# First chunk of the input projection: modulation accumulated as columns, weight splits between the norm pairs, products by pair of row tiles

## What is computed

```python
mod = jax.nn.silu(c) @ w_ada + b_ada                 # (1, 1024) @ (1024, 3072)
shift, scale, gate = jnp.split(mod, 3, axis=-1)
h = _rmsnorm(x, g_pre) * (1.0 + scale[:, None, :]) + shift[:, None, :]
proj = h @ w_in
...
h_sb = ... * jax.nn.silu(sb_z)
y = jnp.concatenate([h_ml, h_sb], axis=-1) @ w_out
x = x + gate[:, None, :] * _rmsnorm(y, g_post)
```

## Time and profile before

| | |
|---|---|
| device time, median of 3 runs | 3646.36 us (3642.9 to 3648.1) |
| the profiled execution: its own time | 3643.63 us |
| the profiled execution: span | 3641.8 us |
| PE busy | 3490.5 us, 96% |
| PEld / DVE / ACT / POOL busy | 77% / 69% / 53% / 18% |
| mean granted TensorE clock | 0.982 |

### The profile page before, as it was taken

How to read it: one execution, slowest core, us unless ns; L and a number is a source line. 1 busy time by engine, 2 the same in 40 slices (tenths; PEclk the granted TensorE clock), 3 DMA queues, 4 the chain that set the end, 5 groups by cost and what they waited for, 6 DMA issues and landing times. The chain is left out here.

```text
span 3641.8 us, 66405 instructions
## 1 busy us (share of the span) xinstructions
PE 3490.5 (96%) x24179; PEld 2821.4 (77%) x24179; DVE 2497.0 (69%) x3508; ACT 1945.8 (53%) x4047; POOL 639.7 (18%) x676
## 2 busy tenths in 40 slices
PE   6998999999999989989999999899999999799998
PEld 4776888999999968867776777677777777688887
DVE  4664445434588862339897999799889888466665
ACT  4453213222344442227776777677777777355554
POOL 1332333000000014401113111210010001223332
PEclk9998999999999999989999999999999999899999
DMA  8888779767856689960011110210011000666664
GB/s 275 313 300 314 261 246 315 262 226 232 295 179 186 193 271 317 307 208 21 25 47 51 47 33 26 70 42 29 26 59 42 12 17 28 182 201 198 206 201 133
DMA packets 415584, 582.24 MB, mean 160 GB/s; under 512 B 35568, under 2 KB 298096, under 8 KB 414288
## 3 DMA queue, kind: packets, MB, share of 16 engines
q1 hardware_dynamic: 398352, 519.86, 43.7%
q0 software_dynamic: 16960, 58.73, 4.7%
HBM read 393.74 MB, written 184.75 MB: 159 GB/s over the span
## 5 line engine op out<-in xcount | busy, mean ns | idle before, releaser
L1399 DVE TENSOR_TENSOR_SCAN a_prod<-a_keep,a_prod,a_zeros 128x512 f32<-128x512 f32 x896 | 1076.8, 1268 | 87.9 <-ACT a_keep L1315 86.8
L1324 ACT COPY a_turned<-a_rt 128x512 f32<-128x512 f32 x1088 | 547.1, 588 | 257.5 <-PE a_rt L1269 257.2
L1315 ACT ACTIVATE a_keep<-a_z 128x512 f32<-128x512 f32 (+3 forms) x1152 | 555.5, 573 | 43.1 <-PE a_z L1258 42.9
L1269 PEld LDWEIGHTS a_rt<-a_ident,a_prod 128*128 128x128 f32 x4224 | 453.8, 141 | 133.7 <-issue 61.2
L1269 PE MATMUL a_rt<-a_ident,a_prod 128*128 128x128 f32 x4224 | 533.5, 279 | 24.3 <-DVE a_prod L1399 23.4
L1280 PE MATMUL a_acc<-a_turned,a_dw 128*64 128x256 f32 x4352 | 520.0, 380 | 0.7 <-ACT a_osum L1334 0.7
L1280 PEld LDWEIGHTS a_acc<-a_turned,a_dw 128*64 128x64 f32 x4352 | 286.7, 136 | 213.7 <-issue 92.6
L1258 PE MATMUL a_z<-a_khi,a_q 64*128 64x512 f32 (+3 forms) x2304 | 374.0, 403 | 1.3 <-DVE a_xe L1385 0.9
L883 DVE TENSOR_TENSOR p_hlo<-p_wraw,p_hlo 128x1024 fp32r<-128x1024 f32 x85 | 104.5, 1230 | 323.7 <-ACT p_hlo L654 323.7
L654 ACT CAST p_hlo<-p_wraw 128x1024 fp32r<-128x1024 f32 x85 | 89.1, 1048 | 393.2 <-PE p_bank L524 209.6
L1399 DVE TENSOR_TENSOR_SCAN a_prod<-a_keep,a_zeros 128x384 f32<-128x384 f32 (+3 forms) x256 | 227.3, 946 | 77.9 <-POOL a_keep L1216 77.9
(11 more groups left out here) (286 smaller groups left out, 6323.3 us busy)
## 6 DMA issues: line engine op xcount, KB each, us to landing
p_hlo<-scratch_parts SPq DMA_DIRECT2D x130, 512.0 KB, 5.0
p_wraw<-scratch_sums SPq DMA_DIRECT2D x128, 512.0 KB, 6.4
p_aslot<-scratch_parts SPq DMA_DIRECT2D x62, 512.0 KB, 5.0
p_wraw<-in_x SPq DMA_DIRECT2D x8, 2048.0 KB, 12.7
p_u<-in_w_in POOLq DMA_DIRECT2D x64, 256.0 KB, 6.1
scratch_wsums<-p_u POOLq DMA_DIRECT2D x32, 512.0 KB, 6.4
p_hraw<-scratch_sbv POOLq DMA_DIRECT2D x32, 512.0 KB, 7.3
m_xt<-in_x SPq DMA_DIRECT2D x32, 512.0 KB, 4.9
```

The lines of the kernel that those rows point to most:

```text
L1269: last = pe.transpose(rt[k % RB][:, h * QW + i * P:h * QW + (i + 1) * P], prod[:, u % PB, 2 * i + h, kb * P:(kb + 1) * P], ident[:])
L1315: act.activation(keep[:, at % KB, 0:w], z[at % ZB][:, 0:w], ACT.Sigmoid, scale=-Z_SCALE).then_inc(keep_done, 1)
L1324: act.copy(by_head(turned[:, k % TB]), by_head(rt[k % RB][:])).then_inc(turned_done, 1)
L1399: dve.tensor_tensor_scan(prod[:, u % PB, s, 0:w][:, ::-1], keep[:, at % KB, 0:w][:, ::-1], zeros[:, 0:w], first, ALU.mult, ALU.add).then_i ...
```

## The change

- **Modulation as columns.** The matmuls swap their operands: the stationary operand is a 128x128 block of `w_ada`, the moving one a single column of silu(c), and the 16 columns of shift and scale are accumulated over k in bank 7 itself. Four matmuls per row tile become sixteen. The rows, their four copies on ACT (L674), the sixteen column matmuls (L449) and POOL's `one` go away. PE makes row tiles 0 to 5 of the modulation, turns x tiles 0 to 3, makes 6 and 7, and turns 4 to 6, then 7.
- **Weight splits between the pairs.** ACT casts two tiles of `wg` behind each `high_norm`, DVE makes two of `gl` behind each `low_norm`, and DVE's `spread` of a pair is moved ahead of the `low_norm` of the pair before it.
- **Products by pair.** Chunk 0's products run pair by pair over banks 0 to 3 at once. Blocks 0 to 3 are all finished in the last pair; chunk 1 is turned two tiles behind blocks 1 and 3 and two at a time around the gate products, which are split into their high and their low half.
- **Order of loads and waits.** SP loads chunk 1 of x ahead of the small tables, and DVE waits for those tables only at chunk 0's gates.

```diff
@@ -292,6 +291,8 @@
             sp.dma_start(wgraw[:, :, 0:8], w_in[:, C_G:C_G + 8].rearrange("(k p) n -> p k n", p=P), allow_slow_non_contiguous=True).then_inc(wgt_in, 16)
+            sp.wait_ge(xn_done, TPC)
+            sp.dma_start(xt, chunks_of_x(x)[1]).then_inc(x_in, 16)
             sp.dma_start(cw[:], conv_w.rearrange("j (m p) -> p j m", p=P), allow_slow_non_contiguous=True).then_inc(small_in, 16)
@@ -347,8 +348,6 @@
 
-            sp.wait_ge(xn_done, TPC)
-            sp.dma_start(xt, chunks_of_x(x)[1]).then_inc(x_in, 16)
             store_parts(0)
@@ -422,14 +421,14 @@
         def _(pe):
-            pe.wait_ge(csil_ready, 2)
-            rows = lambda b: slice(32 * b, 32 * b + 1)
-            for k in range(KT):
+            pe.wait_ge(csil_ready, 1)
+
+            def modulation(k):
                 pe.wait_ge(wada_in[k], 32)
-                for b in range(4):
-                    last = pe.matmul(bank[6][rows(b), :], csil[:, k:k + 1], wada[:, b // 2, k, b % 2 * CH:(b % 2 + 1) * CH],
-                                     start=k == 0, stop=k == KT - 1, skip_group_check=True)
-                last.then_inc(mod_done, 1)
+                for col in range(2 * KT):
+                    last = pe.matmul(bank[7][:, col:col + 1], wada[:, col // KT, k, col % KT * P:(col % KT + 1) * P], csil[:, k:k + 1],
+                                     start=k == 0 and col == 0, stop=k == KT - 1, skip_group_check=True)
+                return last
 
@@ -442,35 +441,65 @@
 
-            for k in range(RING):
+            for k in range(6):
+                modulation(k)
+            for k in range(4):
                 turn(0, k)
-            pe.wait_ge(row_ready, 5)
-            for k in range(2 * KT):
-                last = pe.matmul(bank[7][:, k:k + 1], mrow[0:1, k * P:(k + 1) * P], one[:], start=True, stop=True)
-            last.then_inc(col_done, 1)
-            turn(0, 6)
+            modulation(6)
+            modulation(7).then_inc(col_done, 1)
+            for k in range(4, 7):
+                turn(0, k)
             pe.wait_ge(col_ready, 3)
             turn(0, 7)
-            for n in range(NCH):
+
+            def gate_products(n, k, low):
+                dst = bank[(BLOCKS * n + 4) % RING]
+                if low:
+                    return pe.matmul(dst[0:8, :], wgt[:, k, 0:8], hlo[:, n % 2, k], start=False, stop=k == KT - 1, skip_group_check=True)
+                return pe.matmul(dst[0:40, :], wgt[:, k], hhi[:, n % 2, k], start=k == 0, stop=False, skip_group_check=True)
+
+            for pair in range(PAIRS):
+                for b in range(4):
+                    f = slice(b * P, (b + 1) * P)
+                    if pair == 0:
+                        pe.wait_ge(a_evac if b % 2 == 0 else v_evac, b // 2 + 1)
+                    for k in (2 * pair, 2 * pair + 1):
+                        if b == 0:
+                            pe.wait_ge(n_lo, pair + 1)
+                            pe.wait_ge(wg_lo, k + 1)
+                        for q, (stationary, moving) in enumerate(((gh[:, k, f], hhi[:, 0, k]), (gh[:, k, f], hlo[:, 0, k]), (gl[:, k, f], hhi[:, 0, k]))):
+                            last = pe.matmul(bank[b][:], stationary, moving, start=k == 0 and q == 0, stop=k == KT - 1 and q == 2)
+                    if pair == PAIRS - 1:
+                        last.then_inc(f_full, 1)
+                        if b % 2:
+                            turn(1, b - 1)
+                            turn(1, b)
+            pe.wait_ge(wgt_step, 3)
+            for k in range(KT):
+                gate_products(0, k, False)
+            for k in (4, 5):
+                turn(1, k)
+            for k in range(KT):
+                last = gate_products(0, k, True)
+            last.then_inc(f_full, 1)
+            for k in (6, 7):
+                turn(1, k)
+            for n in range(1, NCH):
                 for b in range(BLOCKS):
...
                     if b == 4:
-                        if n == 0:
-                            pe.wait_ge(wgt_step, 3)
                         for k in range(KT):
-                            pe.matmul(dst[0:40, :], wgt[:, k], hhi[:, n % 2, k], start=k == 0, stop=False, skip_group_check=True)
+                            gate_products(n, k, False)
                         for k in range(KT):
-                            last = pe.matmul(dst[0:8, :], wgt[:, k, 0:8], hlo[:, n % 2, k], start=False, stop=k == KT - 1, skip_group_check=True)
+                            last = gate_products(n, k, True)
                     else:
...
                                 pe.wait_ge(n_lo, PAIRS * n + k // 2 + 1)
-                            if n == 0 and b == 0:
-                                pe.wait_ge(wg_lo, k + 1)
                             hl = [(gh[:, k, f], hhi[:, n % 2, k]), (gh[:, k, f], hlo[:, n % 2, k]), (gl[:, k, f], hhi[:, n % 2, k])]
@@ -537,7 +566,6 @@
             identity(pool, ident[:], id_ready, 0)
-            pool.memset(one[:], 1.0).then_inc(csil_ready, 1)
             pool.memset(y[:, 1], 0.0).then_inc(wgt_step, 1)
@@ -610,7 +638,7 @@
             act.wait_ge(m_in, 48)
-            act.activation(csig[:], ccol[:], ACT.Sigmoid).then_inc(row_ready, 1)
+            act.activation(csig[:], ccol[:], ACT.Sigmoid).then_inc(csig_ready, 1)
 
@@ -669,16 +697,14 @@
             deviation(0)
-            act.wait_ge(mod_done, KT)
-            for b in range(4):
-                act.copy(mrow[0:1, b * CH:(b + 1) * CH], bank[6][32 * b:32 * b + 1, :]).then_inc(row_ready, 1)
             act.wait_ge(col_ready, 3)
...
                 high_norm(0, pair)
-            act.wait_ge(wg_in, 16)
-            for k in range(KT):
-                act.copy(gh[:, k], wg[:, k]).then_inc(wg_hi, 1)
+                if pair == 0:
+                    act.wait_ge(wg_in, 16)
+                for k in (2 * pair, 2 * pair + 1):
+                    act.copy(gh[:, k], wg[:, k]).then_inc(wg_hi, 1)
             act.wait_ge(wgt_in, 16)
@@ -828,7 +854,7 @@
             dve.wait_ge(m_in, 48)
-            dve.wait_ge(row_ready, 1)
+            dve.wait_ge(csig_ready, 1)
             dve.tensor_tensor(csil[:], csig[:], ccol[:], ALU.mult).then_inc(csil_ready, 1)
@@ -896,15 +922,16 @@
             dve.wait_ge(col_ready, 3)
+            spread(0, 1)
             for pair in range(PAIRS):
-                spread(0, 2 * pair + 1)
+                if pair + 1 < PAIRS:
+                    spread(0, 2 * pair + 3)
                 low_norm(0, pair)
-            for k in range(KT):
-                dve.wait_ge(wg_hi, k + 1)
-                dve.tensor_tensor(gl[:, k], wg[:, k], gh[:, k].bitcast(F32), ALU.subtract).then_inc(wg_lo, 1)
+                for k in (2 * pair, 2 * pair + 1):
+                    dve.wait_ge(wg_hi, k + 1)
+                    dve.tensor_tensor(gl[:, k], wg[:, k], gh[:, k].bitcast(F32), ALU.subtract).then_inc(wg_lo, 1)
             dve.wait_ge(wgt_step, 2)
             dve.tensor_tensor(wgt[:, :, 32:40], wgraw[:, :, 0:8], wgt[:, :, 0:8].bitcast(F32), ALU.subtract).then_inc(wgt_step, 1)
-            dve.wait_ge(small_in, 80)
             for n in range(NCH):
@@ -938,6 +965,7 @@
                     dve.wait_ge(zero_out, 32)
+                    dve.wait_ge(small_in, 80)
                 dve.scalar_tensor_tensor(out=gt[0:8], in0=bank[(BLOCKS * n + 4) % RING][0:8, :], scalar=gbias[:], in1=y[0:8, 1],
```

More of the change, by code:

```diff
@@ L152, in stage_project @@
         ccol, csig, gcol, bcol = sb("ccol", [P, KT]), sb("csig", [P, KT]), sb("gcol", [P, KT]), sb("bcol", [P, 2 * KT])
-        acol, shcol, sc1, one = sb("acol", [P, KT]), sb("shcol", [P, KT]), sb("sc1", [P, KT]), sb("one", [1, 1])
+        acol, shcol, sc1 = sb("acol", [P, KT]), sb("shcol", [P, KT]), sb("sc1", [P, KT])
         ss = sb("ss", [P, TPC])
@@ L160, in stage_project @@
         hraws = [heven[:], hraw[:]]
-        mrow = hraw[0:1, 0:4].rearrange("a k t -> a (k t)")
         wg = wfirst[:, 0, 1]
@@ L225, in stage_project @@
         csil_ready, id_ready = sem("csil_ready"), sem("id_ready")
-        mod_done, row_ready, col_done, col_ready = sem("mod_done"), sem("row_ready"), sem("col_done"), sem("col_ready")
+        csig_ready, col_done, col_ready = sem("csig_ready"), sem("col_done"), sem("col_ready")
         sq_done, var_done, rt_done, r_step, xn_done = sem("sq_done"), sem("var_done"), sem("rt_done"), sem("r_step"), sem("xn_done")
```

## The result

| | before | the changed kernel |
|---|---|---|
| device time, median | 3644.63 us, 4 runs (3642.06 to 3648.10) | 3665.49 us, 4 runs (3664.86 to 3668.72) |
| ratio, 95% interval | | 1.0057 [1.0044, 1.0071] |
| the profiled execution, its span | 3643.63 us, 3641.8 | 3664.86 us, 3663.1 |
| PE / PEld busy | 3490.5 us (96%) / 77% | 3529.2 us (96%) / 2872.3 us (78%) |
| mean granted clock | 0.982 | 0.985 |

The changed kernel is 20.9 us slower; 3670 was forecast. The busy share of PE can't tell the two apart: PE has 39 us more work, and PE's share of the span stays 96%.

What follows compares the result with a forecast made beforehand. PE's first products wait for a chain of modulation, turns and column matmuls, then norms and weight splits. Profiled 3643.6 + 28 - 3 = 3668.6, with the median's 2.7 above it 3671.4, stated as 3670; range 3652 to 3680.

Steps and rivals of the forecast that it cites:

- the sum 28 - 3 = 25: Columns taken by DVE 28 us later, less 3 us kept of PE's earlier start on the products.
- Step 1, the level of the clock: Modulation as columns: PE's clock stays low for all eight row tiles, 6.8 us each, making the columns 28 us later.
- Step 1, the price: Modulation as columns: each one-column pass costs 0.213 us at the low level, with ends of 0.114 and 0.228.
- Step 2, PE's start: Chunk 0's first products: PE starts 3.9 us after `col_ready` instead of 13.3, 9.4 us sooner.
- Step 2, what is kept: At chunk 1, fed by ACT and DVE: 3 us of PE's earlier start stays, ends nothing and 9.4.
- the 9.4: Microseconds by which PE was to start chunk 0's products sooner after `col_ready`; only 3 were expected to stay.
- The gaps that I expected around chunk 1: PE waits at chunk 1's turns, between 90 and 110 us: the old wait moved to chunk 0's end.
- Small edits: Chunk 1 of x loaded ahead of the tables, `one` removed, DVE's wait moved: each worth nothing.
- A clock that rises: Rival: PE's clock rises during the modulation, columns 3.8 us later, less 3; 3647 us, no change; chance 0.09.
- a load with one price at either level: Rival: modulation loads cost about 0.114 us at either clock level; 3648 us, no change; chance 0.06.
- Faster by PE's head start: Rival: clock rises, chunk 1's turns find banks free, the whole 9.4 us stays; 3638.5 us; chance 0.05.

Runs made afterwards that it cites:

- the fast start: The changed kernel with five 512-column matmuls into an unused bank ahead of the modulation, so PE's clock is up when it begins; 3663.78 us, ratio 1.0048.
- The columns alone: The kernel before with only the modulation as columns (changed PE, ACT and POOL code up to `col_ready`); 3671.88 us, ratio 1.0072.
- Splits alone: The kernel before with the weight splits between the pairs, DVE's `spread` moved ahead and the new load order; rows and block order stay; 3640.53 us, ratio 0.9988.
- all but the columns: The changed kernel with the modulation as rows, ACT's row copies and the column matmuls put back as before; 3640.66 us, ratio 0.9988.
- early turns with products by pair: Splits alone with x tiles 0 to 3 turned between the last modulation row tiles, column matmuls following each row copy, and chunk 0's products by pair; 3637.54 us, 0.9978.

## Why the prediction was right, and where it was off

**The mechanism held.** Of the sum 28 - 3 = 25, the profiles gave 27.0 - 6.1 = 20.9, and the runs 20.9.

*Step 1, the level of the clock.* Low for all eight row tiles, as I took it: 0.214 us a pass. The kernel that begins on a fast clock shows that this is no accident of the start. The fall at 41.25 behind a stretch of one-column passes was the right row to reason from, though that stretch was only 3.70 us long and eight turns stood between it and the fall; the fast start is what made it certain.

*Step 1, the price.* 0.213 was taken from other kinds of float32 instruction at the low level and from a scaling of the earlier trace rows; 0.214 was measured, so 256 passes cost 55 us. The scaling was partly luck: 0.84 ns for each of 128 columns is 107 ns only if the rest of the 89 ns that 8 columns take is left out. With it the line gives 0.19 us, which is how long such a load lasts at the full level (0.19); 0.107 is how far they are apart. It was the earlier trace rows that carried the price. The columns were taken at 66.96 where I had 67.6; most of the difference is PE's start, 8.85 instead of 9.52. The columns alone cost 27.6 in the runs.

*Step 2, PE's start.* I had 3.9 us behind `col_ready`, and it came at 4.0: 9.3 us sooner. As I had it, PE doesn't starve within chunk 0 in the changed kernel: its list of waits has only the 0.9 there.

*Step 2, what is kept.* This is the term that was mis-sized. I kept 3 us; it was 4.5 at chunk 0's gates and 6.1 at the end of the first pass. The chain was rightly named, but each link was priced a little long. Counted from `col_ready`:

| | forecast | changed kernel |
|---|---|---|
| measuring of chunk 1 starts | 12.6 | 11.7 |
| DVE scales chunk 1 | 19 | 17.9 |
| DVE evicts block 0 | 28 | 26.3 |
| last `low_norm` of chunk 1 ends | 46 | 43.6 |

(In the second row of the forecast the 22 of before is 62.45 - 40.48, so 4.1 was already gained there and not 3.) The 4.5 and the 6.1 lie within the ends of 0 and 9.4 that I had given. The remaining 1.6 come in chunks 1 to 7, and whose they are is open. Splits alone shows them too (+46.7 to +278.1, against +50.8 to +284.2), but all but the columns has only 0.5 of them (+46.6 to +279.5), and the kernel with the fast start, splits and all, takes 0.7 longer over these chunks than the kernel before. The runs without the columns put the whole gain at 3.6 and 4.2 us.

*Where the rest of the 9.4 went.* The gaps that I expected around chunk 1 are there. One, of 2.0 us, is at a turn; the other, of 1.6, is at chunk 1's first product and not at a turn. When the products by pair stand alone, two such gaps of 1.3 and 1.6 us match the 2.8 us that this kernel is behind at chunk 0's gates (+53.6 against +50.8). But the cause that I gave for them, DVE's token sums ahead of the eviction of block 0, is not borne out: moving the sums away made the kernel slower. What the rows show in its place is that with the sums moved DVE waits for ACT at that eviction.

*Small edits.* The order of loads is worth nothing, as forecast.

*The rivals.* (The 3.8 of the first is 3.6 by its own terms, 43.5 plus 0.1 less 40.01; no conclusion hangs on it.) A clock that rises (3647) and a load with one price at either level (3648) are both refuted by the kernel with the fast start. For the load the Trainium skill ("TensorE: Matmul & The Clock Gate", section "LDWEIGHTS") gives 107 ns for 128 columns without regard to the clock; here they are 0.105 us apart at the full level and 0.21 at the low one, so for these float32 loads it agrees at the full level alone. *Faster by PE's head start* (3638.5) needed the clock and the whole 9.4, and neither came: 4.5 was left at chunk 0's gates. That a gain is in the rest of the change is true all the same: without the columns it is 3.6 us faster.

The later stages are shifted by 20 to 21 us and not by the 25 of the sum: the second stage's first scan starts at 1647.76 against 1627.55, and the spans end 21.3 apart.

## What to carry to other kernels

In a float32 matrix-vector product like this one, keep the vector as the stationary operand and move the matrix in wide rows. At the low clock a row tile of 128x2048 cost 1.9 us so and 6.8 the other way, and at the full one 1.04 and 3.4 (32 passes of 0.105). A row tile is loaded in 2.6 us, so the rows hid behind the loads at either level and the columns at neither. That was far more than the 6 us of row copies and column matmuls it saved. When a change makes an engine start earlier, follow the gain to the next work that has the same producers, and price it there. When two profiles differ by a microsecond or two, look first at whether PE's clock stood at the same level at the same work. Before taking a queued operation out of an engine's way, look whether it fills a wait, and who stands behind its result.

## What the runs showed of the hardware

- With PE doing nothing but float32 loads of 128 columns with one moving column, busy without a gap, the clock still fell from 1.00 to 0.50 (at 14.5 us in the kernel with the fast start), and the passes ran low up to their end at 63.3 us. It fell in the middle of such passes in early turns with products by pair too, at about 35.8. Products of 512 columns brought it back in 4.4 us (68.1 to 72.5), as in the kernel before.
- The price of such a pass follows the clock: 0.105 us at 1.00 and 0.214 us at 0.50.
- The clock's level at the same work differs between executions: with the modulation as rows the last row tile took 1.04 us in one profile and 1.89 in four others, and that moved `acol` by up to 1.7 us.
- The granted clock of the page says nothing of the stretch ahead of its first record: 1.00 stands beside passes of 0.21 us, and the mean of the changed kernel (0.985) is above that of the kernel before (0.982), although its PE ran at the low level up to 75.8 us.
